# Stick-breaking attention on 64-wide tiles, the sample's part in one stage with the delta inputs, and semaphores cleared inside other stages

## The reference

```python
def stick_breaking(q, k, v, q_pos, k_pos, bias):          # 4 heads of 64
    z = jnp.einsum('bqhd,bkhd->bhqk', q, k).astype(jnp.float32) * (q.shape[-1] ** -0.5)
    z = z + bias.astype(jnp.float32)[None, :, None, None]
    mask = k_pos[None, :] < q_pos[:, None]
    log_beta = jax.nn.log_sigmoid(z)
    log_keep = jnp.where(mask, jax.nn.log_sigmoid(-z), 0.0)
    suffix = lax.cumsum(log_keep, axis=3, reverse=True)
    after = jnp.concatenate([suffix[..., 1:], jnp.zeros_like(suffix[..., :1])], axis=-1)
    att = jnp.where(mask, jnp.exp(log_beta + after), 0.0)
    return jnp.einsum('bhqk,bkhd->bqhd', att.astype(v.dtype), v)
...
    qd = l2_normalize(qd.reshape(b, t, H_D, DK_D))
    kd = l2_normalize(kd.reshape(b, t, H_D, DK_D))
    beta = jax.nn.sigmoid(bd.astype(jnp.float32))
    g = -jnp.exp(P['dn_a_log'][l].astype(jnp.float32)) * jax.nn.softplus(
        ad.astype(jnp.float32) + P['dn_dt_bias'][l].astype(jnp.float32))
```

## Time and profile before

| | us |
|---|---|
| median of three runs | 1748.67 |
| the profiled execution | 1755.58 |
| its span, first to last instruction | 1753.5 |
| PE busy in it | 1436.3 (82%) |
| DVE, ACT, POOL busy | 743.3, 460.6, 208.5 |

### The profile page before, as it was taken

The page is one execution under the profiler, slowest core; times in us unless marked ns, Lnnn a source line. Parts: engine busy times, 40 slices in busy tenths (PEclk is TensorE's granted clock), DMA queues, the critical chain, the costliest instruction groups (busy, mean ns, idle before and its releaser), DMA issues. The chain is left out here.

```text
span 1753.5 us, 24143 instructions
## 1 busy us (share of the span) xinstructions
PE 1436.3 (82%) x9399; PEld 986.1 (56%) x9400; DVE 743.3 (42%) x1137; ACT 460.6 (26%) x943; POOL 208.5 (12%) x206
## 2 busy tenths in 40 slices
PE   5999899679996699759968998977983698999910
PEld 2554899655565488648733996866851233333300
DVE  3230563356631366356621101335646343344358
ACT  1111424156642533142101113423210111111122
POOL 0000000023310463000000000000000111111046
PEclk9999999789985699579989998998986799999965
DMA  8100111130000300030063103513016396882154
GB/s 303 54 37 30 38 53 49 35 96 1 0 1 3 111 4 4 8 127 1 1 216 96 37 13 140 196 49 127 1 53 262 122 347 250 311 311 82 63 196 148
DMA packets 76895, 174.25 MB, mean 99 GB/s; under 512 B 12884, under 2 KB 40667, under 8 KB 70387
## 3 DMA queue, kind: packets, MB, share of 16 engines
q1 hardware_dynamic: 67339, 137.73, 22.4%
q0 software_dynamic: 5856, 21.24, 3.5%
q10 hardware_dynamic: 3600, 13.90, 2.0%
HBM read 142.27 MB, written 30.66 MB: 99 GB/s over the span
## 5 line engine op out<-in xcount | busy, mean ns | idle before, releaser
L2981 PE MATMUL bank<-arena,hT 128*64 x384 | 172.3, 602 | 11.3 <-DVE hT L3090 5.0
L2982 PE MATMUL bank<-arena,hT 128*64 128x512 f32 x384 | 172.3, 603 | 0.0
L466 PE MATMUL bank<-arena,hT 128*128 128x512 f32 (+3 forms) x432 | 140.1, 478 | 0.0
L2981 PEld LDWEIGHTS bank<-arena,hT 128*64 128x64 f32 x384 | 53.2, 139 | 123.3 <-issue 123.3
L3100 DVE COPY arena<-arena 128x4096 f32 x24 | 55.1, 2295 | 130.0 <-PE bank L2982 118.0
L466 PEld LDWEIGHTS bank<-arena,hT 128*128 128x128 f32 (+1 forms) x432 | 68.2, 183 | 72.2 <-issue 72.1
L2096 PE MATMUL bank<-hT_rest,f_w_high 128*128 128x352 f32 x288 | 93.6, 325 | 0.0
L2949 POOL DMA_INDIRECT hT<-tokens,row_token x24 | 40.4, 1682 | 447.3 <-PE bank L2966 228.2
L3005 PE MATMUL bank<-arena,hT 128*64 x192 | 87.5, 599 | 2.4 <-ACT hT L3045 2.4
L3007 PE MATMUL bank<-arena,hT 128*64 128x512 f32 x192 | 87.5, 599 | 0.0
L2095 PE MATMUL bank<-o_w_high,o_s_high 128*128 128x512 f32 (+1 forms) x144 | 57.6, 400 | 18.7 <-DVE o_w_low L2215 18.7
(11 more groups left out here) (489 smaller groups left out, 3081.1 us busy)
## 6 DMA issues: line engine op xcount, KB each, us to landing
arena<-in_ex_wg_dram SPq DMA_DIRECT2D x16, 1024.0 KB, 8.0
arena<-in_ex_wu_dram SPq DMA_DIRECT2D x16, 1024.0 KB, 10.8
arena<-in_ex_wd_dram SPq DMA_DIRECT2D x16, 1024.0 KB, 12.8
expert_rows<-hT ACTq DMA_DIRECT2D x24, 512.0 KB, 5.5
arena<-in_cache_mem_k_dram SPq DMA_DIRECT2D x8, 1024.0 KB, 5.0
arena<-in_w_in_dram SPq DMA_DIRECT2D x12, 512.0 KB, 3.9
h<-in_x_prompt_dram SPq DMA_DIRECT2D x8, 512.0 KB, 9.0
arena<-in_w_in_dram SPq DMA_DIRECT2D x2, 2048.0 KB, 17.3
```

Source lines behind the costliest of these rows:

```text
L466: last = nc.tensor.matmul(ps[bank][0:r, 0:n], hT[:, k, i * P:i * P + r], wt[:, k, col:col + n], start=(k == 0), stop=(k == KC - 1))
L2981: nc.tensor.matmul(ps[UPB[u % 2]][0:LR, :], xT[:, u % 2, k, 0:LR], gate_up_of[:, bass.ds(slot, 1), :, k, :].rearrange("p a g f -> p (a g) ...
L2982: last = nc.tensor.matmul(ps[UPB[u % 2]][LR:P, :], xT[:, u % 2, k, LR:P], wB_gate_up[:, :, k, :], start=(k == 0), stop=(k == KC - 1))
```

## The change

1. **Prompt's sticks.** A head's scores are now one product on 64 rows of the array (head 0 of a pair on the upper, head 1 on the lower half, each half into its own PSUM bank), so the zero-padded copies on POOL go. A head's values are one product with 64 columns of weights, into its half of the output partitions. Four products of 128 columns stand where two of 256 stood, each with a semaphore increment. The order of heads in the ring is 0, 2, 1, 3, and the output needs one copy, not two.
2. **Sample's sticks and delta inputs in one stage**, their instructions interleaved on each engine. Scores and values of the sample have 32-wide weights (one head each, zero-padded for the other sequences) and the keys or values as the moving side; queries lie on partitions, so the suffix becomes one scan along the free axis on DVE, over reversed columns. Attention is turned by three transposes before the values. The squares move from ACT to DVE (two) and POOL (two), and the four table loads with them go.
3. **Semaphores** are kept in groups; SP clears a group at the end of its list in a later stage (`stage_stick_prompt`, `stage_delta`, both `stage_residual`), and the three blocks of `renew_semaphores` go.

```diff
-    def renew_semaphores():
-        with nc.Block() as block:
-            @block.sync
-            def _(sp):
-                for x in held:
-                    sp.sem_clear(x)
...
+    def clear_semaphores(sp):
+        for x in groups[0][0]:
+            sp.sem_clear(x)
+    psum = ctx.enter_context(nc.psum_tensor("bank", [P, 8 * 512], F32))
+    c.ps = [psum[:, b * 512:(b + 1) * 512] for b in range(8)]
@@ stage_stick_prompt, scores
-                    last = nc.tensor.matmul(ps[n % 2][:, pair * 256:(pair + 1) * 256], kT[:, pair, kb * P:(kb + 1) * P],
-                                            qz[:, qb % 2, 2 * pair:2 * pair + 2, :].rearrange("p h q -> p (h q)"),
-                                            start=True, stop=True)
-                last.then_inc(score, 1)
+                    for half in range(2):
+                        r = slice(half * DH, (half + 1) * DH)
+                        nc.tensor.matmul(ps[2 * (n % 2) + half][:, pair * P:(pair + 1) * P],
+                                         kT[r, pair, kb * P:(kb + 1) * P], qT[r, pair, qb * P:(qb + 1) * P],
+                                         start=True, stop=True).then_inc(score, 1)
@@ values
-                    last = nc.tensor.matmul(ps[4 + qb % 2][:, pair * 256:(pair + 1) * 256],
-                                            vtok[:, kb, pair * P:(pair + 1) * P],
-                                            att[:, n % 2, 2 * pair:2 * pair + 2, :].rearrange("p h q -> p (h q)"),
...
+                        nc.tensor.matmul(ps[6 + qb % 2][r, pair * P:(pair + 1) * P], vtok[:, kb, h * DH:(h + 1) * DH],
+                                         att[:, n % 2, 2 * half + pair, :], start=(kb == qb and pair == 0), stop=(kb == 0),
+                                         skip_group_check=True).then_inc(pv, 1)
@@ stage_sample_and_inputs, PE (new)
+            for b in range(4):
+                turn(b)
+            decays()
+            for b in range(4, DB):
+                turn(b)
+            square_sums(0)
...
+                    nc.tensor.matmul(ps[4][h * NS:(h + 1) * NS, 0:NK], qz[:, h, b, :], kTs[:, b, h // 2, :],
+                                     start=(b == 0), stop=(b == DB - 1), skip_group_check=True)
...
+                    last = nc.tensor.matmul(ps[4][h * NS:(h + 1) * NS, new], qz[:, h, b, :], kT[:, h // 2, SEQ:TOK],
+                                            start=False, stop=(b == DB - 1), skip_group_check=True)
...
+            square_sums(1)
+            square_sums(2)
+            pe.wait_ge(att_ok, 1)
...
+            square_sums(3)
...
+                    last = nc.tensor.matmul(ps[2][h * NS:(h + 1) * NS, 0:DH], attz[:, g % NPG, h, g // NPG, :],
+                                            Vp[:, g, h * DH:(h + 1) * DH], start=False, stop=(g == NPAGES - 1),
@@ ACT (new)
+            inverse_norms(0)
+            act.wait_ge(z_ok, 1)
+            link(nc.scalar.activation(t, z, ACT.Abs))
+            link(nc.scalar.activation(t, t, ACT.Exp, scale=-1.0))
+            nc.scalar.activation(t, t, ACT.Ln, bias=1.0).then_inc(soft, 1)
+            inverse_norms(1)
+            act.wait_ge(arg_ok, 1)
+            nc.scalar.activation(z, z, ACT.Exp).then_inc(exp_ok, 1)
+            inverse_norms(2)
...
+            inverse_norms(3)
+            act.wait_ge(pv, HEADS)
+            nc.scalar.copy(out, ps[2][:, 0:DH]).then_inc(pv_ok, 1)
@@ DVE (new)
+            link(nc.vector.tensor_tensor_scan(sums, K("ones")[:, 0:1].to_broadcast([P, NA]), sp_, 0.0, ALU.mult, ALU.add))
+            nc.vector.tensor_tensor(z, z, sums[:, ::-1], ALU.subtract).then_inc(arg_ok, 1)
```

More of the change, by code:

```diff
@@ L954, in scores @@
                 qb, kb = steps[n]
-                pe.wait_ge(q_ready, 2 * qb + 2)
                 if n >= 2:
@@ L1030, in _ @@
             dve.wait_ge(bias_in, 16)
-            for h in range(HEADS):
-                ins = nc.vector.tensor_scalar(bias[:, h, :], K("ones"), c.A("sb")[:, h:h + 1], None, ALU.mult)
+            for n, h in enumerate(order):
+                ins = nc.vector.tensor_scalar(bias[:, n, :], K("ones"), c.A("sb")[:, h:h + 1], None, ALU.mult)
                 ins.then_inc(bias_ok, 1)
@@ L1276, in _, with turn @@
-            last.then_inc(gpe, 1)
-            for n in range(4):
-                pe.wait_ge(sq_ok, n + 1)
+            def turn(b):
+                if b >= 4:
+                    pe.wait_ge(kT_ok if b % 2 == 0 else kT_ok2, b // 2 - 1)
+                for pair in range(2):
+                    for g in range(NPG):
+                        last = nc.tensor.transpose(ps[b % 4][:, pair * NK + g * P:pair * NK + (g + 1) * P],
+                                                   Kp[:, b * NPG + g, pair * P:(pair + 1) * P], K("ident"))
+                last.then_inc(turned, 1)
@@ new lines, in decays @@
+            def decays():
+                pe.wait_ge(st_ok, 1)
+                pe.wait_ge(gd, 5)
+                for q, (a, b) in enumerate((("cum64", "cum4"), ("blk64", "blk4"))):
+                    nc.tensor.matmul(ps[5][:, q * NC:q * NC + NT * HEADS], K(a), c.g[:, 0:NT, :].rearrange("p i h -> p (i h)"),
+                                     start=True, stop=True)
+                    last = nc.tensor.matmul(ps[5][0:NS, q * NC + NT * HEADS:(q + 1) * NC], K(b, NS, NS), c.g[0:NS, NT, :],
+                                            start=True, stop=True)
+                last.then_inc(gpe, 1)
@@ new lines, in _ @@
+            for g in range(NPAGES):
+                for h in range(HEADS):
+                    last = nc.tensor.matmul(ps[2][h * NS:(h + 1) * NS, 0:DH], attz[:, g % NPG, h, g // NPG, :],
+                                            Vp[:, g, h * DH:(h + 1) * DH], start=False, stop=(g == NPAGES - 1),
+                                            skip_group_check=True)
+                    if g == NPAGES - 1:
+                        last.then_inc(pv, 1)
+            pe.wait_ge(pv_ok, 1)
+            nc.tensor.transpose(ps[0][0:DH, 0:P], out, K("ident")).then_inc(out_turned, 1)
@@ L1306, in _, with inverse_norms @@
             act.wait_ge(eps_ok, 1)
[L1307 to L1311 removed]
+            def inverse_norms(n):
                 for g in range(GRP):
@@ L1360, in stage_delta @@
+            unit_rows(3)
+            dve.wait_ge(out_turned, 1)
+            ov = ps[0][0:DH, 0:P].rearrange("p (c h q) -> p c h q", c=2, h=2)
+            for half in range(2):
+                nc.vector.tensor_copy(oT[half * DH:(half + 1) * DH, 0:2, SEQ:TOK], ov[:, :, half, :]).then_inc(out_ok, 1)
 def stage_delta(c):
```

382 lines of the change are left out of this document (169 added, 213 removed).

## The result

The changed kernel takes 1684.64 us (median of four runs, 1682.91 to 1687.17) beside 1749.34 for the kernel before on the same chip: ratio 0.963, 95% interval 0.961 to 0.965. It is 64.7 us faster; 54.7 had been forecast (1694, range 1680 to 1714). The profiled execution took 1684.20 us, span 1682.4.

What follows compares the result with a forecast made beforehand. A two-step ring through PE, DVE and ACT paces the prompt's sticks; the sample's stretch is one engine-to-engine chain. Semaphores 10.4 + sticks 7.8 + merged stage 36.5 = 54.7 us off 1748.67: 1694 us, range 1680 to 1714.

Steps and rivals of the forecast that it cites:

- rival (c): Stage borders: the clears are not covered and SP holds up the borders, 10.4 us lost, 1704 us; chance 0.04.
- PE's piece of the ring: Prompt's sticks: PE's part of the two-step dependence loop, suffix start to scores, falls from 3.61 to 3.29 us.
- the next ring: Prompt's sticks: the loop through DVE and ACT alone, 3.32 us a step, limits the pace next.
- the mean gained in 27 steps: Prompt's sticks: 0.25 us saved in each of the 27 steps that follow no diagonal, 6.8 us in all.
- Rival (a): Prompt's sticks: half-array products do not overlap, or drain longer; sticks lose 5 us, total 1707 us; chance 0.12.
- the prediction's own sign: Merged stage: the forecast counts as wrong if this stage lasts outside 36 to 59 us.
- decays: Merged stage, first link: 7.9 us before plus 1.5 for DVE's new work ahead of it, 9.4 us.
- norms ahead of the exponential: Merged stage: ACT's second round of inverse norms, with a mask, stands ahead of the exponential, 4.3 us.
- values: Merged stage: 136 records of 64 columns on four column tiles at 0.05 us each, 6.8 us.
- (b): Merged stage: PE stays at 1.2 GHz and 32-wide weights come one at a time; 59 us, total 1710 us; chance 0.22.
- (d): Prompt's sticks: granted clock falls to 1.2 GHz as PE pauses and streams less; slower than before, 1777 us; chance 0.04.
- the second sign of being wrong: Stages the change does not touch: the forecast counts as wrong if one moves by more than 2 us.

Runs made afterwards that it cites:

- the run head by head: Changed kernel with the merged stage's 32 small score and 128 value products ordered head by head, not taking turns on column tiles: 1687.59 us, ratio 0.965.
- The two kernels with one shift: Changed kernel with POOL's squares and memset waiting until the decays' sums are read, 1678.79 us; or with DVE's first square behind the decays' chain, 1682.74 us.

## Why the prediction was right, and where it was not

**Semaphores** (-10.4): exact to 0.1 us. The clears are hidden, rival (c) is out.

**Prompt's sticks** (-7.8, measured -9.8): the mechanism was right. PE's piece of the ring was forecast at 3.29 us and is 3.21; a pair of steps at 6.79 and is 6.74 to 6.80; the next ring at 3.32 and is 3.31. The term that was mis-sized is the mean gained in 27 steps: 0.25 taken, 0.31 measured (8.3 us). It is nothing in the second interval of a block, 0.80 in the third and 0.21 in the later ones (0.20 forecast); the prediction saw that there was more to be had behind a diagonal, and allowed too little for it. The start gave 0.65 (0.6), the end 0.9 (0.4). Rival (a) is out: four products take 0.43 us. The rule of the Trainium skill, "TensorEngine Tiling (Array Packing)", section Key Properties, on the drain at a change of tiling mode agrees with the trace: 0.56 us at the three changes in a step of 3.14 (0.54 was forecast).

**Merged stage** (-36.5, measured -44.6): by the prediction's own sign this part was wrong, since 34.76 us lie below the 36 that it had as lower end. The sum was off by 8.1 us, with errors in both directions. That the total still fell within the range, 4.6 us above its lower end, is in part luck: the decays' 2.0 us were lost against the other terms. By links, forecast and measured: decays 9.4 / 11.4, transposes 3.4 / 3.4, squares 3.5 / 2.7, scores 5.8 / 4.4, bias to scan 4.0 / 3.9, norms ahead of the exponential 4.3 / 1.5, turning the weights 4.2 / 3.5, values 6.8 / 2.4, end 1.2 / 1.1. Three terms made it:

- Values, 4.4 us too long. I took 0.05 us a record, between L1616's pace and L1703's; it is 0.0155. L1703 goes to one column tile, which the run head by head prices at 0.053 us a record (6.75 us); what the prediction overlooked is that L1703 also ran at a granted clock of 0.50, and there cost twice that, 0.107. The small scores were the same error, 1.4 us.
- Norms, 2.8 us too long. I put ACT's second round ahead of the exponential in full; the profile shows two of its three thirds beside the mask, the scan and the subtraction on DVE, in ACT's wait. A list on an engine is not a delay while that engine waits anyway.
- Decays, 2.0 us too short. I added 1.5 us for DVE's new work at the price of an idle neighbour; POOL's square beside it made the first square 2.89 us instead of 1.25, and POOL's memset the two copies 1.31 instead of 0.40. The two kernels with one shift read the decays at 9.6 and 9.7.

What merging alone gave, as against the new forms of the products and the squares moved off ACT, is not shown: no run puts the two new parts one behind the other.

The scan took 0.76 us where a plain operation of its size (L1358) took 0.46. That agrees with the half throughput that the Trainium skill states ("DVE: opcode table, instruction layouts, handler registers and perf-mode slots", section 6), if the time that does not grow with the columns is taken off both: 32 and 288 columns take 0.19 and 0.46 us (L1355, L1358), which leaves an estimated 0.16, and 0.60 against 0.30.

**Rivals (b) and (d)**: (b) is out, the clock was 0.85. (d) did not come: the clock is 1.00 in the sticks from 380.7 on. But the run without a suffix product shows falls of the clock there. **An untouched stage** moved by more than 2 us, the second sign of being wrong that the prediction had named: cross, 6.5. A window near its start before and one after:

```profile
1075.00:1090.00 15.00, 13.96 (x88) 11.38 (x88) 4.49 (x8) 5.32 (x16) 0.00 (x0) 0.77 0.37 140
```

```profile
1016.00:1031.00 15.00, 14.14 (x112) 12.47 (x111) 5.01 (x8) 6.42 (x17) 0.00 (x0) 1.00 0.56 210
```

In the first, PE runs at 0.77 and 140 GB/s are moved; in the second at 1.00, with 210. The three touched parts alone make up the medians' difference, and the profiled execution of before lay 6.9 us above its median, so this most likely belongs to that execution and not to the change; why its clock was lower and its loads slower was not tried.

## What to carry to other kernels

Where a step's pace is a ring of dependences, work taken off one engine is paid only as far as the next ring: look at the order of the lists before, or together with, the products, and count every ring (here about 3.38, 3.31 and PE's own 3.14). Let small products take turns on the array's column tiles, and price them by a row that does the same, at the same granted clock. Before work is put on an idle POOL, look whether DVE's critical chain runs at that moment.

## What was not expected of the hardware

- In the meetings read here, a DVE operation with all its operands in SBUF and one of POOL's do not run beside each other: whichever begins later waits for the other's end (2.89 us for 1.25, 1.09 for 0.17, 1.11 for 0.69, POOL's 2.89 for 1.95; POOL's memset holds two small copies in the same way, 1.31 for 0.40). A copy out of PSUM is not held, nor are 35 adds with one operand in PSUM.
- 128 records of 64 columns that take turns on four 32-wide column tiles take 1.99 us, 6.75 when one tile's records follow each other, both at a granted clock of 1.00.
- The granted clock fell to 1.2 GHz three times in a stage in which PE had been busy two thirds of the time at 2.4 (0.52 to 0.57 in three windows of 3.5 to 4 us).
